# A two-layer and one-block transformer forward pass on one core: dummy matmuls at the start, a split last output, and a reordered recurrent block

## The chip, the cores and the metric

The kernel runs on one core of one Trainium2 chip. The metric is the device time of one execution, in microseconds (us); lower is better. All times below are from profiled or timed executions of the kernel before the change.

## The reference

The input is 256 tokens of width 1024, in float32. Two layers and a further block follow each other. Cut to the part that the change touches:

```
def rg_lru_block(x, w_in, b_in, conv_w, conv_b, gate_w, gate_b, lam, w_out, b_out):
    u = x @ w_in + b_in
    gate_branch, rec = u[..., :1024], u[..., 1024:]
    rec = causal_depthwise_conv(rec, conv_w, conv_b)          # 4 taps
    gl = (block-diagonal product of rec with gate_w) + gate_b # 4 blocks of 256
    r_gate, i_gate = sigmoid(gl[0]), sigmoid(gl[1])
    log_a = -8 * r_gate * softplus(-lam)
    a = exp(log_a);  mult = sqrt(-expm1(2 * log_a))
    h = linear_recurrence(a, mult * (i_gate * rec))           # along the tokens
    return (gelu(gate_branch) * h) @ w_out + b_out

layer 0:  h = x + rg_lru_block(rms_norm(x));  h = h + swiglu_ffn(rms_norm(h))
layer 1:  h = h + stick_breaking_attention(rms_norm(h));  h = h + swiglu_ffn(rms_norm(h))
block 2:  two mixers on rms_norm(h), merged;  h = h + merged @ w_out
          h = h + (p @ w_ple) * sigmoid(h @ w_ple_gate)       # the output
```

## The kernel before

Every weight matrix is read once, in chunks of 128x2048 numbers (1 MB). A chunk is loaded in two halves from SP's queue into `raw`, which has two slots (`RAWS = 2`): the load of chunk c waits until VectorE has finished the same half of chunk c-2 (`lo_dve`). ScalarE copies a half to `whi` (rounded to fp32r; `split_part`, L983), VectorE writes the rest, `wlo = raw - whi` (L1503), and TensorE multiplies with three matmuls per tile (hi x hi, hi x lo, lo x hi). `whi` and `wlo` have four slots. `split_alone` is a split in which VectorE makes the copy too (L1710). Each engine's program is written out by hand, in order; semaphores join them.

Chunks 0 to 3 are `rec` (the recurrent half of `w_in`), 4 `gates_a`, 5 `branch_a`, 6 `gates_b`, 7 to 9 `branch_b`, 10 to 13 `lru_out`, 14 on the first feed-forward part. TensorE takes them in this order. Around the change:

- Start: `x` lands in two halves (`s_x`); squares and roots give a factor for each token; VectorE writes it on diagonals (`diag`, L1561); TensorE multiplies `h` with them, which transposes and scales at once (L583, eight traced matmuls for each of four groups j); ScalarE and VectorE make `xhi` (L1015) and `xlo` (L1535); chunk 0 then goes through TensorE in pairs of k (L448 to L450).
- Parameters: small rows are transposed (`parameters`, L589 and L590), and VectorE computes from them (L1626 to L1644).
- Recurrent block, for each of four groups j of 256 channels: ScalarE `last_tap` (L1079), VectorE `convolve` (L1668, L1677), ScalarE `rec_hi` (L1087), VectorE `conv_lo` (L1690); then for pairs of groups the gates' products on TensorE, ScalarE sigmoids (L1100), Exp and Tanh (`gate_decay`, L1110 and L1116), Sqrt (`gate_root`, L1123), Gelu (`branch_gelu`, L1131); VectorE `gated_input` (L1696), `decay_factor` (L1701), `scan` (L1716, L1719), `output` (L1726); ScalarE `y_hi_of` (L1138), VectorE `output_lo` (L1731). TensorE's `outputs_wide` for `lru_out` waits for `y_lo`, and its second chunk writes banks that the Gelus of groups 2 and 3 read.
- `output_bias` on GpSimd's queue adds `b_out` to `h` with two accumulating DMAs of 512 KB (L430), after `rec` chunk 3.
- End: the last product (`ple_gate`) is followed by Sigmoid (L1481), a product and a sum on VectorE (L2265, L2266) and the DMA to `out` (L419), for tiles of 128x512.

ScalarE's functions come from table sets; a change of set is an instruction of its own (ACT_TABLE_LOAD).

## Time and profile before

| | us |
|---|---|
| median of 3 runs | 847.23 (846.73 to 847.96) |
| the profiled execution's own time | 846.38 |
| its span, from the first to the last instruction | 844.6 |
| TensorE busy in it | 827.6 (98%) |
| VectorE busy | 573.3 (68%) |
| ScalarE busy | 475.5 (56%) |
| DMA | 148.31 MB, mean 176 GB/s |

The span is the stretch that the trace shows; 1.8 us of the execution's time lie around it. Busy shares are averages over the whole span, and the change touches the first 90 us and the last 20.

### The profile page before, as it was taken

Reading aid. Unit: us, or ns where it says so; the run is one execution under the profiler, and the core shown is the slowest. Engines: PE = TensorE matmul, PEld = TensorE weight load, DVE = VectorE, ACT = ScalarE, POOL = GpSimd, SP = SyncE. Lnnn points to the kernel's source line nnn. Section 1 sums busy time; section 2 is a strip of 40 time slices with the busy share of each in tenths; the row PEclk is TensorE's granted clock in tenths of the full one; section 3 lists DMA queues with packets and bytes.
Section 4 is the critical chain, followed back from the end, with each engine's and each line's share of the span. In section 5 each row is a group of like instructions: output and inputs, shape, how many; then the busy total and the mean of one; then the engine's idle time right before and its main releaser. Section 6 shows DMA issues by size and latency. Waiting matters only on the chain.

```text
span 844.6 us, 12734 instructions
## 1 busy us (share of the span) xinstructions
PE 827.6 (98%) x5093; PEld 735.4 (87%) x5093; DVE 573.3 (68%) x825; ACT 475.5 (56%) x674; POOL 2.1 (0%) x6
## 2 busy tenths in 40 slices
PE   5998999999999999999999999999999999999997
PEld 5997888888888899998888888888999999999886
DVE  5979785665644577775765665555757789888763
ACT  6699684444434566655664444435654846577441
POOL 0000000000000000000000000000000000000000
PEclk9999999999999999999999999999999999999999
DMA  8674688656555464344676556555554364444531
GB/s 279 209 208 159 209 254 262 198 177 196 178 193 179 150 200 139 119 142 130 214 230 195 180 177 195 190 186 177 168 180 136 115 199 126 128 147 142 189 119 50
DMA packets 124307, 148.31 MB, mean 176 GB/s; under 512 B 6217, under 2 KB 100953, under 8 KB 124121
## 3 DMA queue, kind: packets, MB, share of 16 engines
q1 hardware_dynamic: 122584, 144.73, 54.0%
q0 software_dynamic: 288, 1.05, 0.8%
q10 hardware_dynamic: 1376, 1.72, 0.7%
q8 instruction: 41, 0.67, 0.3%
q14 instruction: 18, 0.14, 0.1%
HBM read 146.41 MB, written 2.63 MB: 176 GB/s over the span
## 4 chain that ended last, share of the span: by engine, by line
PE 85%; DVE 6%; ACT 5%; DMA 3%; issue 1%; SPq 0%; ACTq 0%; DVEq 0%
PE bank L506 18%; PE bank L508 18%; PE bank L507 18%; PE bank L448 7%; PE bank L449 6%; PE bank L450 6%; DVE wlo L1503 2%; DMA raw<-in_lru_w_in 2%; PE bank L863 2%; PE bank L455 1%; PE bank L457 1%; PE bank L456 1%; ACT whi L983 1%; PE bank L657 1%; PE bank L517 1%
## 5 line engine op out<-in xcount | busy, mean ns | idle before, releaser
L1503 DVE TENSOR_TENSOR wlo<-raw,whi 128x1024 fp32r<-128x1024 f32 (+1 forms) x268 | 314.8, 1212 | 103.0 <-ACT whi L983 102.4
L983 ACT ACTIVATE whi<-raw 128x1024 fp32r<-128x1024 f32 (+1 forms) x266 | 267.0, 1048 | 177.7 <-PE bank L508 103.1
L448 PE MATMUL bank<-xhi,whi 128*128 128x256 f32 x576 | 165.1, 287 | 0.2 <-issue 0.2
L450 PE MATMUL bank<-xhi,wlo 128*128 128x256 f32 x576 | 162.9, 283 | 0.0
L449 PE MATMUL bank<-xlo,whi 128*128 128x256 f32 x576 | 162.9, 283 | 0.0
L506 PE MATMUL bank<-whi,xhi 128*128 128x512 f32 x384 | 151.6, 395 | 0.3
L508 PE MATMUL bank<-whi,xlo 128*128 128x512 f32 x384 | 149.8, 390 | 0.0
L507 PE MATMUL bank<-wlo,xhi 128*128 128x512 f32 x384 | 149.5, 389 | 0.0
L448 PEld LDWEIGHTS bank<-xhi,whi 128*128 128x128 f32 x576 | 110.4, 192 | 1.8 <-issue 1.2
L449 PEld LDWEIGHTS bank<-xlo,whi 128*128 128x128 f32 x576 | 110.5, 192 | 0.1
L450 PEld LDWEIGHTS bank<-xhi,wlo 128*128 128x128 f32 x576 | 110.4, 192 | 0.0
L508 PEld LDWEIGHTS bank<-whi,xlo 128*128 128x128 f32 x384 | 72.1, 188 | 15.3
L506 PEld LDWEIGHTS bank<-whi,xhi 128*128 128x128 f32 x384 | 72.1, 188 | 15.2 <-issue 0.9
L507 PEld LDWEIGHTS bank<-wlo,xhi 128*128 128x128 f32 x384 | 72.2, 188 | 14.4
L506 PE MATMUL bank<-whi,a_ghi 128*128 128x512 f32 x176 | 69.1, 392 | 0.0
L508 PE MATMUL bank<-whi,a_glo 128*128 128x512 f32 x176 | 68.6, 390 | 0.0
L507 PE MATMUL bank<-wlo,a_ghi 128*128 128x512 f32 x176 | 68.5, 389 | 0.0
L1216 ACT ACTIVATE a_sg<-bank,stat 128x256 f32<-128x256 f32 x44 | 18.5, 471 | 65.2 <-PE bank L508 65.2
L1803 DVE SCALAR_TENSOR_TENSOR a_gt<-bank,stat,a_sg 128x256 f32<-128x256 f32 x44 | 19.3, 480 | 47.6 <-ACT a_sg L1216 45.1
L508 PEld LDWEIGHTS bank<-whi,a_glo 128*128 128x128 f32 x176 | 33.0, 188 | 7.0
L506 PEld LDWEIGHTS bank<-whi,a_ghi 128*128 128x128 f32 x176 | 33.0, 188 | 6.7
L507 PEld LDWEIGHTS bank<-wlo,a_ghi 128*128 128x128 f32 x176 | 33.1, 188 | 6.6
(313 smaller groups left out, 1176.6 us busy)
## 6 DMA issues: line engine op xcount, KB each, us to landing
raw<-in_ffn_w_in SPq DMA_DIRECT2D x176, 256.0 KB, 3.6
raw<-in_w_in SPq DMA_DIRECT2D x48, 512.0 KB, 4.7
raw<-in_ffn_w_out SPq DMA_DIRECT2D x44, 512.0 KB, 4.1
raw<-in_attn_w_qkv SPq DMA_DIRECT2D x24, 512.0 KB, 4.6
raw<-in_lru_w_in SPq DMA_DIRECT2D x14, 512.0 KB, 5.3
raw<-in_lru_w_out SPq DMA_DIRECT2D x8, 512.0 KB, 4.0
raw<-in_attn_w_o SPq DMA_DIRECT2D x8, 512.0 KB, 3.9
raw<-in_w_out SPq DMA_DIRECT2D x8, 512.0 KB, 4.6
```

Source lines behind the costliest of these rows:

```text
L448: nc.tensor.matmul(dst, wh, hi, start=start, stop=False, skip_group_check=shared)
L449: nc.tensor.matmul(dst, wh, lo, start=False, stop=False, skip_group_check=shared)
L450: return nc.tensor.matmul(dst, wl, hi, start=False, stop=stop, skip_group_check=shared)
L455: nc.tensor.matmul(dst, hi, wh, start=start, stop=False)
L506: nc.tensor.matmul(dst, hi, wh, start=start, stop=False)
L507: nc.tensor.matmul(dst, hi, wl, start=False, stop=False)
L508: return nc.tensor.matmul(dst, lo, wh, start=False, stop=stop)
L863: last = nc.tensor.matmul(dst, k[:, u * P:(u + 1) * P], queries, start=True, stop=True)
L983: nc.scalar.activation(whi[:, c % RING, part], raw[:, c % RAWS, part], ACT.Copy).then_inc(hi_done, 1)
L1216: nc.scalar.activation(sg[:, q % 2, a, :], bank[(b0 + 2 * q + a) % 4][:, 0:S], ACT.Sigmoid, scale=stat[:, 10 * xn + 8 + a:10 * xn + 9 + a] ...
L1503: nc.vector.tensor_tensor(wlo[:, c % RING, part], raw[:, c % RAWS, part], whi[:, c % RING, part].bitcast(F32), ALU.subtract).then_inc(lo_d ...
L1803: marks.append(mark(nc.vector.scalar_tensor_tensor(out=gt[:, q % 2, a, :], in0=bank[(b0 + 2 * q + a) % 4][:, 0:S], scalar=tok(xn, a), in1= ...
```

## The change

What it does:

- TensorE runs 10 dummy products of a tile of ones before the identity lands and 7 more before the diagonals are ready (`keep_clock`; in the trace a float32 product shows as two matmuls). Of the four transposing groups the last runs between chunk 0's first and second pair of k. The squares at the start are shared out anew: ScalarE takes the first 128 tokens, VectorE the others, each as a half lands.
- Of the 1216 KB of constants only the 50 KB of `bucket` are loaded at their old place; the others (1 MB) go behind the fourth chunk of `ffn_in0`, and `p_tok` behind `gates_b`. `bound_constants` moves into the feed-forward part, and VectorE computes the parameters behind the first half of chunk 1.
- In the recurrent block, Sqrt for all four groups comes once, behind the second `gate_decay`, and Gelu's table stays for all four groups. VectorE alone splits chunks 7 and 8, and ScalarE copies chunk 10 (10 was VectorE's). ScalarE's copy of chunk 6 moves ahead of `last_tap(3)`, and the bucket copy moves to ScalarE.
- The two bias DMAs wait for `rec` chunk 2, not 3.
- The last 128x512 tile of `ple_gate` is computed, activated, added and stored in two halves of 256 columns.

The diff, cut to its core:

```diff
                     if layer == 0 and c == 3:
+                        sp.dma_start(const[:, 256:CONST["bucket"]], t["consts"][:, 256:CONST["bucket"]])\
+                            .then_inc(s_const, 16)
...
-            sp.dma_start(p_tok[:, :, :], t["p_2"][0, 0].rearrange("(a p) d -> p a d", p=P))\
-                .then_inc(s_p, 16)
-            sp.dma_start(const[:, 256:], t["consts"][:, 256:]).then_inc(s_const, 16)
+            bucket = slice(CONST["bucket"], CONST["bucket"] + 384)
+            sp.dma_start(const[0:33, bucket], t["consts"][0:33, bucket]).then_inc(s_bucket, 16)
             stage("rec", lambda c: w_in[4 + c], 2)
...
-                pool.wait_ge(chunk_done, STAGES["rec"][0] + 3 + 5)
+                pool.wait_ge(chunk_done, STAGES["rec"][0] + 2 + 5)
...
+            def keep_clock(n):
+
+                for _ in range(n):
+                    nc.tensor.matmul(bank[5][:, 0:P], rs[:, 0:P], rs[:, 0:P], start=True, stop=True)
+
+            pe.wait_ge(warm_ready, 1)
+            keep_clock(10)
+            pe.wait_ge(s_ident, 16)
+            pe.wait_ge(s_gain, 16)
+            nc.tensor.transpose(bank[4][:, 0:16], prow[0:16, 0, :], ident[0:16, 0:16]).then_inc(gain_t, 1)
+            keep_clock(7)
+            pe.wait_ge(tok_ready, 1)
+            for j in range(3):
+                first_transposes(j)
...
-            columns_part(c0, b0, xhi, xlo, 0, 4, x_lo, 0)
+            columns_part(c0, b0, xhi, xlo, 0, 2, x_lo, 0)
+            first_transposes(3)
+            columns_part(c0, b0, xhi, xlo, 2, 4, x_lo, 0)
             parameters()
             columns_part(c0, b0, xhi, xlo, 4, DT, x_lo, 0)
...
+            def gate_half(c, half):
+
+                dst = bank[4 + half][:, 0:S]
+                for k in range(4):
+                    kk = 4 * (c - 2) + k
+                    xh, xl = xhi[:, kk, P:], xlo[:, kk, P:]
+                    wh, wl = (w[:, (c0 + c) % RING, k * WIDE + half * S:k * WIDE + (half + 1) * S] for w in (whi, wlo))
+                    nc.tensor.matmul(dst, xh, wh, start=kk == 0, stop=False)
+                    nc.tensor.matmul(dst, xh, wl, start=False, stop=False)
+                    last = nc.tensor.matmul(dst, xl, wh, start=False, stop=kk == DT - 1)
+                return last
...
+            nc.scalar.preload_act_table_set("sigmoid_and_others")
             last_tap(0)
             split(3)
             rec_hi(0)
             last_tap(1)
+            act.wait_ge(bkt_t, 1)
+            nc.scalar.activation(bucket_bias[:, :], bank[7][0:8, 0:384], ACT.Copy).then_inc(bkt_done, 1)
             split(4)
             rec_hi(1)
+            act.wait_ge(bkt_done, 1)
+            act.dma_start(bias_dram, bucket_bias[:, :]).then_inc(bkt_out, 16)
             last_tap(2)
             split(5)
             rec_hi(2)
+            split(6)
             last_tap(3)
-            act.wait_ge(bkt_done, 1)
-            act.dma_start(bias_dram, bucket_bias[:, :]).then_inc(bkt_out, 16)
-            split(6)
-            nc.scalar.preload_act_table_set("sigmoid_and_others")
             gate_sigmoids("gates_a", 0)
+            rec_hi(3)
             nc.scalar.preload_act_table_set("exp_and_others")
-            rec_hi(3)
-            split(7)
             gate_decay(0)
-            gate_root(0)
-            split(8)
             nc.scalar.preload_act_table_set("sigmoid_and_others")
             gate_sigmoids("gates_b", 2)
+            act.wait_ge(hi_done, parts_done(8, 2))
             split(9)
             gate_decay(2)
+            gate_root(0)
+            gate_root(2)
             nc.scalar.preload_act_table_set("gelu_apprx_tanh_and_others")
             branch_gelu(STAGES["branch_a"][0], 0)
             c0 = STAGES["branch_b"][0]
             branch_gelu(c0, 1)
+            split(10)
             act.wait_ge(bkt_out, 16)
             y_hi_of(0)
             y_hi_of(1)
-            gate_root(2)
-            act.wait_ge(hi_done, parts_done(10, 2))
             split(11)
-            nc.scalar.preload_act_table_set("gelu_apprx_tanh_and_others")
             branch_gelu(c0 + 1, 2)
             branch_gelu(c0 + 2, 3)
...
+            split_part(1, 0)
             dve.wait_ge(par_t, 1)
...
-            split(1)
+            split_part(1, 1)
             split(2)
...
-            lru_constants()
-            dve.wait_ge(bkt_t, 1)
-            nc.vector.tensor_copy(bucket_bias[:, :], bank[7][0:8, 0:384]).then_inc(bkt_done, 1)
             convolve(1)
             split(4)
             conv_lo(1)
             convolve(2)
             split(5)
             conv_lo(2)
+            lru_constants()
             convolve(3)
             split(6)
             conv_lo(3)
-            split(7)
+            split_alone(7)
             gated_input(0)
             gated_input(1)
             decay_factor(0)
             decay_factor(1)
-            scan(0)
-            split(8)
-            scan(1)
+            split_alone(8)
             gated_input(2)
             gated_input(3)
             split(9)
-            split_alone(10)
             decay_factor(2)
             decay_factor(3)
+            scan(0)
             output(0)
+            scan(1)
             output(1)
+            split_part(10, 0)
             output_lo(0)
             output_lo(1)
+            split_part(10, 1)
             scan(2)
...
+                    if n and a:
+                        for half in range(2):
+                            part = slice(half * S, (half + 1) * S)
+                            cols = slice(WIDE + half * S, WIDE + (half + 1) * S)
+                            dve.wait_ge(pg_sig, 4 + half)
+                            link(nc.vector.tensor_tensor(xg[:, 1, part], xg[:, 1, part], ple[:, 1, cols], ALU.mult))
+                            nc.vector.tensor_tensor(h[:, 1, cols], h[:, 1, cols], xg[:, 1, part], ALU.add)\
+                                .then_inc(fin_ready, 1)
+                        continue
```

The rows below are the program order, first of **ScalarE** from the third `rec_hi` to the gates' Exp and Tanh (a_rchi is `rec_hi`, a_rc<-bank `last_tap`, whi<-raw a chunk's copy, a_rg and a_ig the sigmoids, then a_av_lru Exp and a_rg Tanh). Before:

```order
L1087 ACTIVATE a_rchi<-a_rc 128x512
L1079 ACTIVATE a_rc<-bank,small,par 128x256 x2
L1151 DMA bias_scratch<-a_bucket_bias 8x384
L983 ACTIVATE whi<-raw 128x1024 x2
L1153 ACT_TABLE_LOAD
L1100 ACTIVATE a_rg<-bank,par 128x256 x4
L1100 ACTIVATE a_ig<-bank,par 128x256 x4
L1155 ACT_TABLE_LOAD
L1087 ACTIVATE a_rchi<-a_rc 128x512
L983 ACTIVATE whi<-raw 128x1024 x2
L1110 ACTIVATE a_av_lru<-a_rg,small 128x256 x4
L1116 ACTIVATE a_rg<-a_rg,small 128x256 x4
```

And in the changed kernel:

```order
L1131 ACTIVATE a_rchi<-a_rc 128x512
L1026 ACTIVATE whi<-raw 128x1024 x2
L1123 ACTIVATE a_rc<-bank,small,par 128x256 x2
L1144 ACTIVATE a_rg<-bank,par 128x256 x4
L1144 ACTIVATE a_ig<-bank,par 128x256 x4
L1131 ACTIVATE a_rchi<-a_rc 128x512
L1202 ACT_TABLE_LOAD
L1154 ACTIVATE a_av_lru<-a_rg,small 128x256 x4
L1160 ACTIVATE a_rg<-a_rg,small 128x256 x4
L1204 ACT_TABLE_LOAD
L1144 ACTIVATE a_rg<-bank,par 128x256 x4
```

Chunk 6's copy now stands ahead of the fourth `last_tap` instead of behind it, the table load between them is gone, and so is chunk 7's copy ahead of Exp; the second gates' sigmoids follow at once, without Sqrts ahead of them.

**VectorE** behind the last `convolve` (wlo is the rest of a chunk, CAST a chunk's copy on this engine, a_rclo `conv_lo`, a_ig `gated_input`, then `decay_factor`, a_rg and the a_ig behind it `scan`). Before:

```order
L1503 TENSOR_TENSOR wlo<-raw,whi 128x1024 x2
L1690 TENSOR_TENSOR a_rclo<-a_rc,a_rchi 128x512
L1503 TENSOR_TENSOR wlo<-raw,whi 128x1024 x2
L1696 TENSOR_TENSOR a_ig<-a_ig,a_rc 128x512 x2
L1701 SCALAR_TENSOR_TENSOR a_ig<-a_av_lru,a_ig 128x512 x2
L1716 TENSOR_TENSOR a_rg<-a_rg,a_ig 128x512
L1719 SCALAR_TENSOR_TENSOR a_ig<-a_av_lru,a_rg 128x256 x2
L1503 TENSOR_TENSOR wlo<-raw,whi 128x1024 x2
L1716 TENSOR_TENSOR a_rg<-a_rg,a_ig 128x512
L1719 SCALAR_TENSOR_TENSOR a_ig<-a_av_lru,a_rg 128x256 x2
L1696 TENSOR_TENSOR a_ig<-a_ig,a_rc 128x512 x2
L1503 TENSOR_TENSOR wlo<-raw,whi 128x1024 x2
```

And in the changed kernel:

```order
L1558 TENSOR_TENSOR wlo<-raw,whi 128x1024 x2
L1757 TENSOR_TENSOR a_rclo<-a_rc,a_rchi 128x512
L1777 CAST whi<-raw 128x1024
L1558 TENSOR_TENSOR wlo<-raw,whi 128x1024
L1777 CAST whi<-raw 128x1024
L1558 TENSOR_TENSOR wlo<-raw,whi 128x1024
L1763 TENSOR_TENSOR a_ig<-a_ig,a_rc 128x512 x2
L1768 SCALAR_TENSOR_TENSOR a_ig<-a_av_lru,a_ig 128x512 x2
L1777 CAST whi<-raw 128x1024
L1558 TENSOR_TENSOR wlo<-raw,whi 128x1024
L1777 CAST whi<-raw 128x1024
L1558 TENSOR_TENSOR wlo<-raw,whi 128x1024
```

Chunks 7 and 8 now each bring two CASTs into VectorE's order, and the two scans have moved away, behind the rows shown.


## Rows read from the trace of the kernel before

**Rows 1.** The page: busy us, share of the span, instructions.

```profile
PE 827.6 (98%) x5093; PEld 735.4 (87%) x5093; DVE 573.3 (68%) x825; ACT 475.5 (56%) x674; POOL 2.1 (0%) x6
```

**Rows 2.** Timeline of TensorE: start us, us, what, count, [idle before <-releaser].

```profile
8.64 5.39 PE L583 MATMUL bank<-diag,h 128*128 128x128 f32 x32 [2.54 <-DVE diag L1561]
...
20.46 0.36 PE L448 MATMUL bank<-xhi,whi 128*128 128x256 f32 x1 [0.23 <-issue]
...
75.65 0.47 PE L506 MATMUL bank<-whi,a_yhi 128*128 128x512 f32 x1 [1.76 <-DVE a_ylo L1731]
...
82.88 0.47 PE L506 MATMUL bank<-whi,a_yhi 128*128 128x512 f32 x1 [1.51 <-ACT a_gel L1131]
```

**Rows 3.** The chain that ended last, at the start: start us, us, what.

```profile
1.23 5.32 DMA h<-in_x
...
8.64 2.09 PE bank L583 x8
10.82 0.85 ACT xhi L1015 x2
11.77 0.88 DVE xlo L1535 x2
```

**Rows 4.** Only L583: stretch, us, busy (count) of PE and PEld, PEclk, DMA share, GB/s.

```profile
9.10:11.10 2.00, 2.00 (x11) 2.00 (x11) 1.00 0.37 120
12.20:13.60 1.40, 1.40 (x15) 1.40 (x14) 1.00 1.08 322
```

**Rows 5.** The same of all lines, PE, PEld, DVE, ACT, POOL.

```profile
30.00:40.00 10.00, 10.00 (x86) 10.00 (x85) 9.73 (x26) 5.10 (x8) 0.48 (x1) 1.00 0.55 182
825.00:835.00 10.00, 10.00 (x46) 8.29 (x45) 3.08 (x5) 1.20 (x2) 0.00 (x0) 1.00 0.15 54
```

**Rows 6.** Timeline of VectorE.

```profile
17.20 0.28 DVE L1626 COPY par<-bank 128x122 f32<-128x122 f32 x1 [0.40 <-PE bank L590]
19.15 2.35 DVE L1503 TENSOR_TENSOR wlo<-raw,whi 128x1024 fp32r<-128x1024 f32 x2
...
24.34 0.16 DVE L1668 TENSOR_TENSOR a_rc<-a_rc,diag 128x6 f32<-128x6 f32 x1
...
42.66 2.43 DVE L1677 SCALAR_TENSOR_TENSOR a_rc<-bank,par,a_rc 128x255 f32<-128x255 f32 x6
45.01 2.36 DVE L1503 TENSOR_TENSOR wlo<-raw,whi 128x1024 fp32r<-128x1024 f32 x2
...
58.52 1.27 DVE L1719 TENSOR_TENSOR_SCAN a_ig<-a_av_lru,a_rg 128x256 f32<-128x256 f32 x2
...
67.86 0.69 DVE L1710 CAST whi<-raw 128x1024 fp32r<-128x1024 f32 x1
```

**Rows 7.** DMA of 42 to 44 us: queue, packets, MB, share of 16 engines.

```profile
q0 software_dynamic: 78, 0.32, 105.8%
```

**Rows 8.** The chain that ended last, in the recurrent block.

```profile
41.98 9.35 DMA raw<-in_lru_w_in
```

**Rows 9.** DMA of 40 to 41.5 us: issues, KB each, median us to landing.

```profile
h<-in_lru_b_out POOLq DMA_DIRECT2D x2, 512.0 KB, 8.0
raw<-in_lru_w_in SPq DMA_DIRECT2D x1, 512.0 KB, 7.4
```

**Rows 10.** Timeline of ScalarE in the recurrent block.

```profile
54.04 1.71 ACT L1116 ACTIVATE a_rg<-a_rg,small 128x256 f32<-128x256 f32 x4
55.77 1.28 ACT L1123 ACT_TABLE_LOAD   x1
...
81.06 1.57 ACT L1131 ACTIVATE a_gel<-bank,par 128x256 f32<-128x256 f32 x4
```

**Rows 11.** Timeline of GpSimd's queue.

```profile
39.52 1.90 POOL L430 DMA_DIRECT2D h<-in_lru_b_out  x2 [39.08 <-PE bank L450]
```

**Rows 12.** The chain that ended last, at the end.

```profile
840.08 0.61 ACT xg L1481
841.43 0.69 DVE h L2266
```

More of the change, by code:

```diff
@@ L415, in _ @@
             out_v = out[0].rearrange("(a p) d -> p a d", p=P)
-            for j in range(4):
+            for j in range(3):
                 cols = slice(j // 2 * WIDE, (j // 2 + 1) * WIDE)
@@ L585, in _ @@
                 last.then_inc(chunk_done, 1)
+            pe.wait_ge(warm_ready, 1)
[5 more added lines that the diff above has]
+            pe.wait_ge(tok_ready, 1)
+            for j in range(3):
+                first_transposes(j)
             def parameters():
@@ L958, in _ @@
                         pe.wait_ge(banks_read, b0 + c + a + 1)
+                    if c >= 2 and a == 1:
+                        for half in range(2):
+                            last = gate_half(c, half)
+                            if c == 3 and half == 0:
+                                last.then_inc(pg_mm, 1)
+                        continue
                     last = gate_part(c, a, 0, 4)
@@ L1476, in _ @@
                         act.wait_ge(pg_mm, n + 1)
-                    else:
-                        act.wait_ge(chunk_done, c0 + 2 * n + 1 + 5)
+                    elif n == 0:
+                        act.wait_ge(chunk_done, c0 + 1 + 5)
                     if n:
                         act.wait_ge(fin_ready, a + 1)
+                    if n and a:
+                        for half in range(2):
+                            cols = slice(half * S, (half + 1) * S)
+                            if half:
+                                act.wait_ge(chunk_done, c0 + 3 + 5)
+                            else:
+                                act.wait_ge(pg_mm, 3)
+                            nc.scalar.activation(xg[:, 1, cols], bank[4 + half][:, 0:S], ACT.Sigmoid)\
+                                .then_inc(pg_sig, 1)
+                        continue
                     nc.scalar.activation(xg[:, a, :], bank[(b0 + 2 * n + a) % 4][:, :], ACT.Sigmoid)\
@@ L1844, in ffn @@
                         norm_factor(xn)
-                        if layer:
+                        if not layer:
+                            bound_constants()
+                        else:
                             link(nc.vector.tensor_tensor(two_gains, gains("final_norm"), gains("norm_gain"),
@@ L2263, in _ @@
                 for a in range(2):
+                    if n and a:
+                        for half in range(2):
+                            part = slice(half * S, (half + 1) * S)
+                            cols = slice(WIDE + half * S, WIDE + (half + 1) * S)
+                            dve.wait_ge(pg_sig, 4 + half)
+                            link(nc.vector.tensor_tensor(xg[:, 1, part], xg[:, 1, part], ple[:, 1, cols], ALU.mult))
+                            nc.vector.tensor_tensor(h[:, 1, cols], h[:, 1, cols], xg[:, 1, part], ALU.add)\
+                                .then_inc(fin_ready, 1)
+                        continue
                     dve.wait_ge(pg_sig, 2 * n + a + 1)
```

62 lines of the change are left out of this document (39 added, 23 removed).

## The prediction

> **What bounds the kernel now.** The page first: TensorE is busy 98% of the span [rows 1]. So a gain can come only from a stretch in which it waits, from a slower clock, or from the tail behind its last matmul. Its timeline shows these stretches [rows 2]: nothing but one small product before 8.64 us, idle time of 0.23 us at 20.46, 1.76 us at 75.65 (it waits for the first y_lo) and 1.51 us at 82.88 (for the Gelus that read its banks). The chain at the start says what 8.64 rests on: the DMA of x [rows 3], which no edit touches. The transposing products run at two rates. Of L583 alone [rows 4], 11 matmuls touch 2.0 us early on, each 0.42 us long, so one every (2.0 + 0.42) / 11 = 0.22 us; later 15 touch 1.4 us at 0.28 us each, one every 0.11 us. These are the clock's two levels, 1.2 and 2.4 GHz. The PEclk column says 1.00 in both, so the counts are what shows it. After that a 256-column matmul takes (10.0 + 0.28) / 86 = 0.120 us and a 512-column one 0.23 us [rows 5].
>
> **Start.** The ten dummy products are 20 traced matmuls, 20 x 0.21 = 4.3 us from about 1.0 us on; the seven behind the row transposition (about 5.9 us) are 14, so 1.6 us at the fast level, 3.0 at the slow. In before the level rose 15 matmuls, 3.2 us, after 8.64. I expect it up before the diagonals are there. Then the first eight products end at about 9.8 us, where before xhi could start only at 10.82; with ScalarE's 0.85 and VectorE's 0.88 [rows 3] chunk 0 starts at 11.8, where it started at 13.78 = 8.64 + 5.14. It takes 48 x 0.12 = 5.75, the fourth transposing group 0.9 in its midst and the parameters' transpositions 0.5, so it ends at 18.95. Before it ended at about 20.1, the wait at 20.46 behind it. **1.1 us gained** here. In chunk 1 VectorE makes the first half (1.2 us), then the parameter block, 19.15 - 17.20 = 1.95 us [rows 6], then the second half: ready at 20.5, wanted 12 matmuls into the chunk, at 20.4. The 0.36 us of before become 0.1. Chunk 1 ends at 24.7; the bias table takes 0.8 and chunk 2 5.75, to 31.3 us, against 32.9.
>
> If the clock stayed low, the first xhi would come at the old time, the dummies would last to about 9.2 us and hold the transposes back by 0.6, and the fourth group and the waits between would cost in full: chunk 0 would end near 21.7.
>
> **The constants.** 1.2 MB leave the queue ahead of chunk 2, which at the 322 GB/s of the start [rows 4] is 3.5 us of transfer. That is covered now by ScalarE: its copies of chunk 2 wait for the parameters (VectorE, 19.3), four small functions 0.8, copies 2.0, a table 1.28, `last_tap` 0.9, so `convolve(0)` starts at 24.1 against 24.34 [rows 6]. Loaded later, 1 MB goes beside feed-forward chunks of 24 x 0.227 = 5.45 us each, split up to three chunks ahead: some 3 us against 16 us of cover. I take nothing for it; without the cover it would cost up to 3 us.
>
> **The recurrent block up to the fourth group.** `lru_constants` and the bucket copy leave VectorE ahead of `convolve(1)`: it starts 2.54 + 2.28 + 0.6 = 5.4 us behind `convolve(0)` (the first two are 45.01 - 42.47, with the small addition of 0.19 ahead of row 42.66, and two halves' wlo), at 29.5, and ends at 32.05. The first wlo half of chunk 4 is done at 33.2, which releases the first load of chunk 6 (`gates_b`); the second goes 1.1 us later, at 34.4.
>
> This is where the moved wait bites. The bias DMAs were issued 0.9 us after chunk 3 [rows 11], so now at 31.3 + 0.9 = 32.2 us. Each takes 8.0 us to land [rows 9]. Between 42 and 44 us the software queue alone held 105.8% of the engines' time [rows 7], and chunk 7's first half, issued about 1.3 us behind the bias DMAs, took 7.4 us [rows 9], its second, issued at 41.98, 9.35 us [rows 8]. So it landed 41.98 + 9.35 - 39.52 = 11.8 us after the bias DMAs' start. Now chunk 6 stands in chunk 7's place: issued 1.0 and 2.2 us behind them. Its second half lands at 32.2 + 11.5 = 43.7 us (0.3 less, being issued 0.3 sooner behind them). In before ScalarE met chunk 7 off the critical chain of the convolutions; now the copy of chunk 6 stands ahead of `last_tap(3)`: 43.7 + 1.05 + 0.9 gives `convolve(3)` at C = 45.7, against 42.47. What is queued behind: `last_tap(3)`, all gate sigmoids, a_rchi; who waits: VectorE, and through a_rclo TensorE at `gates_b` (2 us).
>
> At that place a rule bears on it. The Trainium skill, DMA: Bandwidth & Descriptors, section "Queues, rings and completion order", says that a DMA engine takes turns between queues, a packet each. The row of 42 to 44 us shows 78 software packets and none of the other queue's; by the rule the halves would come earlier (rival 2).
>
> **From there to the outputs.** Counted from C: VectorE's convolution, chunk 6 and a_rclo 5.4; chunk 7 alone 2 x (0.72 + 1.14) = 3.7 (the CAST and what follows it [rows 6]); four 128x512 operations 2.9; chunk 8's second copy 2.6. That releases ScalarE, which is behind it: chunk 9 2.0, table 1.28, Exp and Tanh 3.45, table 1.28, four Sqrts 2.1, table 1.28, first Gelus 0.8 [rows 10] = 12.2. Then VectorE: y 0.7, a scan 0.7 + 1.3 [rows 6], y 0.7, half a chunk 1.1, y_lo 0.7 = 5.2. With hand-overs y_lo(0) is there at C + 32.1 = 77.8. Before it was 75.55 - 42.47 = 33.1: two table loads (2.6) and two chunks' copies less on ScalarE, but 2.8 us more copying on VectorE now lie in the chain, so it shortens by only 1.0. TensorE, through with `branch_b` at 74.2, stands from there to 77.9.
>
> It then has 5.45 us of work, to 83.3 (before it restarted at 82.88), and needs no Gelu: the fourth one is done at C + 33.6. The second chunk takes it to 88.8, but y_lo(2) comes at C + 43.5 = 89.2 (two scans 4.1, four half chunks less one 3.4, two y 1.4, y_lo 0.7 behind C + 33.9). Before it was there at 82.88 + 5.45 = 88.3. **0.9 us lost.** From here on TensorE is dense in both.
>
> **End.** The halves cost 48 x 0.120 - 24 x 0.227 = +0.3 us of TensorE. The tail, 841.43 + 0.69 - 840.08 = 2.04 us [rows 12], becomes three operations of half width. Bounds for each: half of 0.6 or 0.69, and the whole; I take 0.47 and 0.45 twice, 1.4 us. The last store moves half the bytes; 0.1 for it. **0.4 us gained.**
>
> **Sum.** 846.38 + 0.9 - 0.4 = 846.9 us by the profiled execution. The runs' median of 847.23 lies 0.85 above that one, so **847.7 us** as a median. A measurement of this kernel tells no change from about 0.2%, 1.7 us.
>
> **Rivals.**
> 1. Chunk 6 is not late: the bias DMAs start later, or chunk 6's loads get through before them. For it: only 1 us separates them. Against: chunk 7's load in before, in the same place, was starved. Then C = 41.0 (VectorE-bound: 32.05 + 2.9 + 2.5 + 3.5), y_lo(0) at 73.1, and TensorE is at y_lo(2) at 84.5: 3.8 gained and 0.4 at the end, 843.0. Chance 0.22.
> 2. The queues share, and the second half lands at 41 to 42.5: C = 43 to 44.4, so 1.3 to 2.7 us under the forecast, 845.0 to 846.4; middle 845.7. Chance 0.20, half of it faster by over 0.2%.
> 3. The clock falls in the wait of 3.7 us ahead of y_lo(0). In before the longest wait inside, 1.8 us, left it up. Until it rises again, as at the start for 3.2 us, half the work is lost: 1.6 us, so 849.3, slower. It decides if the wait is long enough for the chip. Chance 0.08. The Trainium skill, TensorE: Matmul & The Clock Gate, section "Why this matters for your kernels", warns of just such gaps between bursts of matmuls.
> 4. The dummies don't raise the clock. Chunk 0 ends 2.8 us later than forecast, the bias DMAs move along with it, and all to y_lo(2) is 2.8 us later: 850.5, slower. For it: a pause of 0.5 us at 5.4 and one of 1 us before 8.64. Chance 0.07.
>
> **Chances.** The forecast has 0.43, its own range 846.4 to 849.3 (C by 1 us either way, the tail by 0.4); of it 0.32 within 0.2%, 0.07 slower, 0.04 faster. Faster: 0.22 + 0.10 + 0.04 = 0.36. Same: 0.32 + 0.10 = 0.42. Slower: 0.07 + 0.08 + 0.07 = 0.22. The range leaves out most of rival 4 and the far ends: 842.4 to 849.7.
>
> **What would show it.** Right: the transposing products at one every 0.11 us from 8.64, chunk 0 starting near 11.8; the bias DMAs issued near 32.2, chunk 6's second half 9 us in flight, ScalarE idle 5 us ahead of its copy; one wait of over 3 us on y_lo, none on a Gelu; a tail of 1.4 us. The forecast is wrong if chunk 6 lands before 41 us, if VectorE reaches chunk 4's wlo over 1 us sooner than 33.2, or if the slow clock lasts into chunk 0.

## Result, and the profile after

The changed kernel takes 849.31 us (median of 11 runs, 848.25 to 850.26), the kernel before 847.23 in the same session: ratio 1.0023, 95% interval 1.0016 to 1.0031, slower by 0.23%. The forecast was 847.7 with 842.4 to 849.7, so the time lies in the range, near its slow end. The profiled execution took 850.19 us with a span of 848.1, so it lies 0.9 above its median, as that of before lay 0.85 below; of the 3.5 us between the two spans, 2.1 stand in the medians.

TensorE's waits of the changed kernel, longest first (where it waited, for whom; total us, times, longest):

```profile
PE bank L458 <- issue: 2.5, 1, 2.5
PE bank L516 <- DVE a_ylo L1798: 2.2, 1, 2.2
PE bank L587 <- DVE rs L1669: 1.1, 1, 1.1
PE bank L594 <- DVE diag L1616: 0.9, 1, 0.9
PE bank L602 <- DMA a_prow<-in_mix_norm: 0.7, 1, 0.7
PE bank L516 <- DVE a_gt L1874: 0.7, 1, 0.7
```

Against [rows 2]: the wait for the Gelus is gone, the one for y_lo(0), the low part of the block's output for group 0, is 2.2 instead of 1.76, and two are new inside the kernel: 2.5 us ahead of `gates_b` (L458), and 0.7 us ahead of the feed-forward's fifth chunk (L516, for a_gt, its first gated product, which VectorE makes from the same banks). Where the waits at `gates_b` and for y_lo(0) come from, the timelines of ScalarE, then of VectorE show (start, duration, operation, in brackets the idle time ahead and its releaser):

```profile
44.55 1.06 ACT L1026 ACTIVATE whi<-raw 128x1024 fp32r<-128x1024 f32 x1 [3.36 <-DMA raw<-in_lru_gate_w]
45.52 1.00 ACT L1123 ACTIVATE a_rc<-bank,small,par 128x256 f32<-128x256 f32 x2
...
46.62 0.17 DVE L1735 TENSOR_TENSOR a_rc<-a_rc,diag 128x6 f32<-128x6 f32 x1 [5.23 <-ACT a_rc L1123]
49.17 2.35 DVE L1558 TENSOR_TENSOR wlo<-raw,whi 128x1024 fp32r<-128x1024 f32 x2
78.17 1.29 DVE L1798 TENSOR_TENSOR a_ylo<-a_rc,a_yhi 128x512 fp32r<-128x512 f32 x2
```

The same two operations of VectorE in the kernel before, the start of `convolve(3)` and y_lo(0):

```profile
42.47 0.16 DVE L1668 TENSOR_TENSOR a_rc<-a_rc,diag 128x6 f32<-128x6 f32 x1
...
74.81 1.29 DVE L1731 TENSOR_TENSOR a_ylo<-a_rc,a_yhi 128x512 fp32r<-128x512 f32 x2
```

ScalarE stands 3.36 us for the second half of chunk 6, the copy takes 1.06, `last_tap(3)` behind it starts at 45.5, `convolve(3)` at 46.62 instead of 42.47. Chunk 6's low parts follow it and are done at 51.5, which is what TensorE waits for at `gates_b`; y_lo(0) starts at 78.17 instead of 74.81. The DMA view says why. Of 33.6 to 35 us, chunk 6's two loads (KB each, median us to landing); under it the queues of 38 to 44 us (packets, MB, share of the engines' time), the software queue being that of the bias transfers:

```profile
raw<-in_lru_gate_w SPq DMA_DIRECT2D x2, 512.0 KB, 8.0
...
q1 hardware_dynamic: 1152, 1.15, 56.8%
q0 software_dynamic: 151, 0.52, 44.2%
```

The clock. TensorE's busy time, matmuls and granted clock by stretch (start:end, us, busy us and count, clock, DMA share, GB/s):

```profile
51.70:55.00 3.30, 3.30 (x16) 0.50 0.91 290
55.20:58.50 3.30, 3.30 (x30) 1.00 0.83 239
79.00:82.40 3.40, 3.40 (x8) 0.50 0.69 202
83.00:86.40 3.40, 3.40 (x17) 1.00 0.53 181
```

After each of the two waits the clock stands at its lower level, 1.2 GHz, for 3.4 us; at the second, 8 matmuls of 512 columns are done in the time of 15 to 17. The output product (`lru_out`), from the start of its first matmul to that of its last, takes 23.8 us, where the kernels without a fall and without a wait for Gelus take 22.1 to 22.5.

The other new wait lies where the constants now load. ScalarE ahead of its copies of the feed-forward's fifth chunk, behind which its sigmoids for a_gt stand in its order; TensorE ahead of that chunk; and the DMA issues of 106 to 112 us, with those of 95 to 104 us last:

```profile
118.55 1.06 ACT L1026 ACTIVATE whi<-raw 128x1024 fp32r<-128x1024 f32 x1 [3.58 <-DMA raw<-in_ffn_w_in]
...
127.32 0.47 PE L516 MATMUL bank<-whi,xhi 128*128 128x512 f32 x1 [0.67 <-DVE a_gt L1874]
...
raw<-in_ffn_w_in SPq DMA_DIRECT2D x6, 256.0 KB, 6.2
const<-in_consts SPq DMA_DIRECT2D x1, 1024.0 KB, 8.0
...
raw<-in_ffn_w_in SPq DMA_DIRECT2D x7, 256.0 KB, 4.2
```

In every trace with the constants loaded at this place ScalarE stands for this load. Where it stood 3.2 us or more (3.58 here, 3.69 in number 12, 3.19 in number 11) TensorE had to wait for a_gt; where it stood 1.1 to 2.3 us, as in the others, it had not.

Start and end of the changed kernel:

```profile
8.45 2.94 PE L594 MATMUL bank<-diag,h 128*128 128x128 f32 x24 [0.93 <-DVE diag L1616]
11.68 0.36 PE L458 MATMUL bank<-xhi,whi 128*128 128x256 f32 x1 [0.29 <-DVEq L1688]
...
844.51 0.38 ACT L1533 ACTIVATE xg<-bank 128x256 f32<-128x256 f32 x1 [0.99 <-PE bank L988]
845.38 0.42 DVE L2340 TENSOR_TENSOR h<-h,xg 128x256 f32<-128x256 f32 x1
```

The transposing products run at one every 0.12 us from the first on (2.94 / 24), and the last sigmoid is followed by 1.29 us to the sum's end (845.38 + 0.42 - 844.51) instead of 2.04 [rows 12].

The sum of the differences between the two profiled spans: lru_out starts 3.35 us later (79.00 against 75.65); through it 0.2 is won (no 1.5 us for the Gelus, 1.3 more for the clock's fall); the a_gt wait and its restart cost 0.9; the halves cost TensorE 0.4; the stretch from the last matmul's end to the span's is 3.6 instead of 4.55, 0.95 shorter. 3.35 - 0.2 + 0.9 + 0.4 - 0.95 = 3.5, the whole difference.

### The profile page after: what moved, and what is told of

It reads as the page before. It is cut to its first block, busy times and chain, and to the rows that moved or that the text cites. A ratio compares the mean times of both kernels' runs of the same rounds, so it can differ in the third digit from the quotient of the medians.

```text
span 848.1 us, 12860 instructions
## 1 busy us (share of the span) xinstructions
PE 835.4 (99%) x5151; PEld 743.3 (88%) x5151; DVE 575.1 (68%) x831; ACT 471.3 (56%) x670; POOL 2.1 (0%) x6
## 4 chain that ended last, share of the span: by engine, by line
PE 84%; DVE 8%; ACT 4%; DMA 3%; issue 1%; SPq 0%; DVEq 0%; ACTq 0%
PE bank L516 17%; PE bank L518 17%; PE bank L517 17%; PE bank L458 7%; PE bank L459 6%; PE bank L460 6%; DVE wlo L1558 3%; PE bank L888 2%; PE bank L465 1%; PE bank L466 1%; PE bank L467 1%; DMA raw<-in_lru_gate_w 1%; PE bank L680 1%; PE bank L527 1%; ACT whi L1026 1%
## 5 line engine op out<-in xcount | busy, mean ns | idle before, releaser
L458 PE MATMUL bank<-xhi,whi 128*128 128x256 f32 x576 | 165.2, 287 | 0.5 <-DVEq L1688 0.3
L516 PE MATMUL bank<-whi,xhi 128*128 128x512 f32 x376 | 148.6, 395 | 1.0 <-DVE a_gt L1874 0.7
L518 PE MATMUL bank<-whi,xlo 128*128 128x512 f32 x376 | 146.7, 390 | 0.0
L517 PE MATMUL bank<-wlo,xhi 128*128 128x512 f32 x376 | 146.5, 390 | 0.0
L458 PEld LDWEIGHTS bank<-xhi,whi 128*128 128x128 f32 x576 | 110.3, 192 | 2.2 <-ACT whi L1026 0.6
L516 PEld LDWEIGHTS bank<-whi,xhi 128*128 128x128 f32 x376 | 70.6, 188 | 15.9 <-ACT whi L1026 1.1
L516 PE MATMUL bank<-whi,a_ghi 128*128 128x512 f32 x176 | 69.1, 392 | 0.0
L516 PEld LDWEIGHTS bank<-whi,a_ghi 128*128 128x128 f32 x176 | 33.0, 188 | 6.7
```

The lines of the kernel that those rows point to most:

```text
L458: nc.tensor.matmul(dst, wh, hi, start=start, stop=False, skip_group_check=shared)
L516: nc.tensor.matmul(dst, hi, wh, start=start, stop=False)
L517: nc.tensor.matmul(dst, hi, wl, start=False, stop=False)
L518: return nc.tensor.matmul(dst, lo, wh, start=False, stop=stop)
```

## Experiments

They ran four kernels at a time on one chip, each beside the kernel before, whose medians there were 847.26 (numbers 1 to 4), 847.47 (5 to 8) and 847.59 (9 to 12). Theory: the moved wait of the bias transfers starves chunk 6 and the rest follows. Rivals: the copies that VectorE took over, the new order of ScalarE's work, the constants, the start and the end.

**1. The wait back at chunk 3 (bias_c3).**

```diff
-                pool.wait_ge(chunk_done, STAGES["rec"][0] + 2 + 5)
+                pool.wait_ge(chunk_done, STAGES["rec"][0] + 3 + 5)
```

> The changed kernel with one wait back in its old place: the two bias transfers wait for recurrent chunk 3 again, not for chunk 2. My theory (the bias transfers, issued at 32.5 us, take the DMA engines from chunk 6's weights, whose second half lands at 44.5; ScalarE stands 3.4 us for it, so convolve(3) starts at 46.6 and not at 42.5, and all of the recurrent chain after it is late): chunk 6's second half lands by 39, convolve(3) starts at 42 to 43.5, TensorE's wait ahead of gates_b is under 0.5 us and the clock doesn't fall there, y_lo(0) comes at 74 to 75.5, and the output product starts there and not at 79.0: 849.3 - 3.5 = 845.8 us (844 to 846.8). The clock may still fall in the wait ahead of y_lo(0), since TensorE is there earlier too. Rival, that VectorE's two more copies and the new order of ScalarE's work make the chain long: convolve(3) comes earlier and y_lo(0) doesn't, 849.3 (848.6 to 850).

Measured 846.71 us, ratio 0.9997 (0.9987 to 1.0007). The 2.5 us wait is gone and y_lo(0) starts 2.6 us earlier, but the transfers now hit chunk 7, and VectorE, which copies it, waits; TensorE stands 3.7 us for y_lo(0), and its clock falls there for 3.4 us:

```profile
51.28 0.69 DVE L1777 CAST whi<-raw 128x1024 fp32r<-128x1024 f32 x1 [2.27 <-DMA raw<-in_lru_w_in]
...
76.39 0.77 PE L516 MATMUL bank<-whi,a_yhi 128*128 128x512 f32 x1 [3.67 <-DVE a_ylo L1798]
```

So the wait is a cause, and its old place is no good one either once VectorE needs chunk 7 itself. I had expected 0.9 us less.

**2. The wait at chunk 6 (bias_c6).**

```diff
-                pool.wait_ge(chunk_done, STAGES["rec"][0] + 2 + 5)
+                pool.wait_ge(chunk_done, STAGES["gates_b"][0] + 5)
```

> The changed kernel with the two bias transfers waiting for chunk 6 (TensorE's second gates, some 54 us), behind every load of the recurrent block's start. My theory: as with the wait at chunk 3, 845.8, and up to 0.5 us less, since chunk 7's and 8's loads are free of them only here if those matter (chunk 7 isn't waited for in the changed kernel's trace, so I take nothing for it): 845.6 (844 to 846.8). If the bias transfers are only put beside another load that is waited for (chunks 9 to 12, of which the changed kernel waits 0.2 us for one): 847 to 849. Rival of the long chain: 849.3.

Measured 843.31 us (842.95 to 843.77), ratio 0.9954 (0.9941 to 0.9966): 6.0 us off the changed kernel by one constant, 2.3 more than the theory gave, since I had overlooked chunk 7. `convolve(3)` and y_lo(0) (VectorE), then TensorE's only wait in the block:

```profile
41.97 0.17 DVE L1735 TENSOR_TENSOR a_rc<-a_rc,diag 128x6 f32<-128x6 f32 x1 [0.34 <-ACT a_rc L1123]
73.52 1.28 DVE L1798 TENSOR_TENSOR a_ylo<-a_rc,a_yhi 128x512 fp32r<-128x512 f32 x2
...
74.35 0.47 PE L516 MATMUL bank<-whi,a_yhi 128*128 128x512 f32 x1 [1.49 <-DVE a_ylo L1798]
```

The clock stays up. The bias transfers now run beside a load for lru_out that nobody is short of: issued at 57.9 us it lands at 67.8.

**3. `last_tap(3)` ahead of `split(6)` (tap_first).**

```diff
+            last_tap(3)
             split(6)
-            last_tap(3)
```

> The changed kernel with last_tap(3) ahead of split(6) on ScalarE again, the bias transfers as in the changed kernel. Chunk 6 still lands at 44.5, but convolve(3) no longer stands behind it: it starts at 42 to 42.5, the low parts of chunk 6 are ready at 46.9, and TensorE's wait ahead of gates_b is gone with the clock's fall there. ScalarE's sigmoids still stand behind chunk 6's high part and come only 0.9 us earlier. If the chain goes by ScalarE's sigmoids (gates_a): y_lo(0) 0.9 us earlier, 848.4. If it goes by VectorE (the copies of chunk 8, for which ScalarE waits 1.3 us at split(9) in the changed kernel, and which come 4 us earlier): y_lo(0) 1.9 to 2.8 us earlier, 847.0 (846.3 to 847.6). If the order was no matter: 849.3.

Measured 847.36 us, ratio 0.9998 (0.9989 to 1.0007), nearest the VectorE case. The wait at `gates_b` is gone though chunk 6 lands as late as before, y_lo(0) starts 2.5 us earlier, and TensorE waits 3.8 us for it. The order of two ScalarE operations was worth 1.9 us, but only because the load between them was late. Here the clock stayed down longer than anywhere else: the granted clock is 0.50 from 75.5 us on, while TensorE still waits, and until 82.2, 6.8 us in all:

```profile
76.50:82.10 5.60, 5.60 (x13) 0.50 0.57 187
83.00:86.40 3.40, 3.40 (x17) 1.00 0.54 183
```

**4. Work in the two waits (fill).** 16 traced matmuls of 128 columns that nobody reads (FILL is 8, and each product shows as two), ahead of `gates_b` and again ahead of lru_out:

```diff
+                if n0:
+                    pe.wait_ge(gate_read, 1)
+                    for _ in range(FILL):
+                        nc.tensor.matmul(bank[4][:, 0:P], rs[:, 0:P], rs[:, 0:P], start=True, stop=True)
...
+            pe.wait_ge(gate_read, 8)
+            for _ in range(FILL):
+                nc.tensor.matmul(bank[7][:, 0:P], rs[:, 0:P], rs[:, 0:P], start=True, stop=True)
```

> The changed kernel with 16 added 128x128 products whose result nobody reads (1.8 us of TensorE) in each of the two waits, ahead of gates_b and ahead of the output product, so that TensorE isn't idle for long there; nothing that anyone waits for is moved. It takes away the clock's two falls alone. If the falls cost what they seem to (each 3.4 us at half speed, 1.7 us of work): the first is taken back in the wait that follows, since TensorE then stands for y_lo(0) anyway; the second comes straight off the end: 849.3 - 1.7 = 847.6 (847.2 to 848.2), and half level shows nowhere but at the start and the end. If the first also holds up ScalarE's sigmoids of gates_b (it waits 0.6 us for TensorE there): 0.6 less, 847.0. If the falls cost nothing: 849.3.

Measured 848.38 us (847.75 to 849.43), ratio 1.0016 (1.0007 to 1.0025): 0.9 us back, of 1.7 expected. The clock is at its upper level in both places, and lru_out takes 22.5 us again. But the first group did not do what I meant: it stood behind a semaphore of its own, so it ran only after a wait of 2.27 us, and put `gates_b` off to 53.2:

```profile
51.40 2.02 PE L642 MATMUL bank<-rs 128*128 128x128 f32 x16 [2.27 <-issue]
...
76.73 1.95 PE L678 MATMUL bank<-rs 128*128 128x128 f32 x16
...
79.00:82.40 3.40, 3.40 (x16) 1.00 0.68 204
```

The third line is the stretch in which the changed kernel did 8. The second fall is thus worth 1.3 us in the profile; the medians show 0.9 for both groups together. The two profiled executions are 2.4 us apart, but 0.9 of that is the wait for a_gt, which this one hasn't.

**5 and 6. The wait alone, in the kernel before (before_bias_c2, before_bias_c6).** There it stood at chunk 3.

```diff
-                pool.wait_ge(chunk_done, STAGES["rec"][0] + 3 + 5)
+                pool.wait_ge(chunk_done, STAGES["rec"][0] + 2 + 5)
```

> The kernel before with one wait changed: the two bias transfers wait for recurrent chunk 2 instead of 3; everything else as before. It tells whether the earlier bias transfers alone lose what the changed kernel lost. My theory: chunk 6's second half lands at 44 to 45 instead of under 41; in this kernel last_tap(3) stands ahead of split(6), so convolve(3) stays at 42.5, but ScalarE waits some 2.4 us for chunk 6, and its sigmoids and all behind them come 1.4 us later (chunk 7, for which it waited 0.96 us, comes earlier). y_lo(0) at 77 instead of 75.65, TensorE waits 3.2 us for it: 848.6; since the clock fell in waits of 2.2 to 3.8 us in the runs so far and not in one of 1.8 us, it falls here, some 1 to 1.7 us more: 850.0 (848.3 to 850.6). Rival, that the early transfers cost only because of the changed kernel's new order: 847.2 (846.8 to 847.6).

Measured 849.85 us, ratio 1.0028 (1.0019 to 1.0037). ScalarE waits 2.6 us for chunk 6's second half, and one of the two waits of TensorE moves: 2.2 us for a_rclo at `gates_b`, after which the clock falls, and 0.6 for y_lo(0). So the earlier bias transfers alone lose what the whole change lost (2.4 us against 2.1).

> The kernel before with the two bias transfers waiting for chunk 6 (TensorE's second gates) instead of recurrent chunk 3; everything else as before. It tells how much of the 843.3 us of the changed kernel with that wait is the wait's and not the change's. My theory: in the kernel before the bias transfers hit chunk 7, for which ScalarE waits 0.96 us at 50.4; without that wait y_lo(0) comes 0.96 us earlier, 1.0 us off TensorE's wait of 1.8: 847.2 - 1.0 = 846.3 (845.8 to 846.8), and the other 3 us of the 843.3 are the change's own. Rival, that the transfers cost the kernel before nothing (the 0.96 us are taken back by another wait of the chain): 847.2. Rival, that nearly all of it is the wait's: 843.5 to 845.

Measured 845.92 us, ratio 0.9981 (0.9973 to 0.999). The wait for y_lo(0) went from 1.8 to 0.6. Of the 3.9 us by which bias_c6 was under the kernel before, 1.5 are thus the wait's place in that kernel and 2.4 the rest of the change. The two don't simply add: by the medians, each against the kernel before of its own session, the rest of the change is worth 0.3 us with the wait at chunk 2 (+2.4 against +2.1), 0.5 at chunk 3 (not clear of noise) and 2.4 at chunk 6.

**7. The end alone (end_only): the kernel before with the last sigmoids, products, sums and stores in halves.**

```diff
+                    if c >= 2 and a == 1:
+                        for half in range(2):
+                            last = gate_half(c, half)
...
-            for j in range(4):
+            for j in range(3):
+            for half in range(2):
+                cols = slice(WIDE + half * S, WIDE + (half + 1) * S)
```

> The kernel before with one part of the change alone: the last gate chunks' second token block in two halves of 256 columns, so that the last sigmoid, product, sum and store are half as wide. Forecast before the result: TensorE 0.3 us longer, the tail 0.6 shorter, the store 0.1: 847.2 - 0.4 = 846.8. From the changed kernel's trace: the last matmul ends 3.6 us before the end instead of 4.55 (0.95 less), TensorE 0.3 us longer: 847.2 - 0.65 = 846.6 (846.3 to 846.9). Rival, that the halves are paid with a wait at the end: 847.2 or more.

Measured 846.55 us, ratio 0.9987 (0.9978 to 0.9996): 0.9 under the 847.47 of its session. The interval runs from 0.3 to 1.9 us, so it shows a gain but can't tell the 0.6 of the traces from the forecast's 0.4.

**8. One more chunk for VectorE (vec9): bias_c6, and chunk 9's high part copied by VectorE too.**

```diff
-            act.wait_ge(hi_done, parts_done(8, 2))
-            split(9)
             gate_decay(2)
...
-            split(9)
+            split_alone(9)
             decay_factor(2)
```

> The changed kernel with the bias transfers waiting for chunk 6 (843.3 us) and one more chunk whose high part VectorE copies: chunk 9, beside 7 and 8. ScalarE's chain is then free of 2.0 us of copies and of the 0.6 us that it waits for VectorE ahead of them. My theory of the chain (from 58 us on it goes by ScalarE: decay, roots, gelu; TensorE stands 1.5 us for y_lo(0) at its end): y_lo(0) comes 2.0 to 2.6 us earlier, at 71 instead of 73.5, TensorE no longer waits for it: 843.3 - 1.5 = 841.8 (841.4 to 842.2). Rival, that VectorE is the chain's bound there (it takes 1.4 us more, ahead of decay_factor(2)): y_lo(0) 1.4 us later, 844.7. Rival, that the low parts of chunk 9 come too late for TensorE (1.4 us later, at 63 us, when TensorE wants them at 65): 843 to 844.

Measured 841.07 us (840.91 to 841.65), ratio 0.9925 (0.9911 to 0.9939), the fastest with number 10. TensorE's wait of 1.5 us is gone, as forecast. y_lo(0) starts at 70.9, and TensorE waits for nothing from 21 us to the feed-forward:

```profile
70.89 1.29 DVE L1797 TENSOR_TENSOR a_ylo<-a_rc,a_yhi 128x512 fp32r<-128x512 f32 x2
...
70.00:76.00 6.00, 6.00 (x38) 1.00 0.52 168
```

**9 to 12. Parts of the change undone in vec9**, where the start and the chain show at the end undisturbed. What they show holds for vec9, where no load of the block is late, and not at once for the changed kernel. They ran in another session than vec9.

9, the 17 products that nobody reads left out (v9_no_dummies):

```diff
-            keep_clock(10)
...
-            keep_clock(7)
```

> The last kernel (bias transfers at chunk 6, VectorE copies chunk 9 too: 841.1 us; TensorE waits for nothing between 21 us and the end of the block, so that what the start loses or gains shows at the end) without the 17 products that nobody reads at TensorE's start. In the kernel before the clock rose 2.8 us after TensorE's first real products; here it would rise at 11.3 us instead of at 4 us, so that the first transposes run at half speed from 8.45 us on: up to 1.5 us lost. The sum on record took 1.1: 842.2 (841.8 to 842.8). If the first chunk's start is set by the arrival of the high and low parts and not by the clock: 841.1 to 841.4.

Measured 842.80 us (842.22 to 843.29), 1.7 over vec9, the far end of what I gave. The first transposing products of this kernel, of vec9, of the kernel before, of before_bias_c2 and of end_only, each with its duration:

```profile
8.57 5.38 PE L594 MATMUL bank<-diag,h 128*128 128x128 f32 x24 [2.41 <-DVE diag L1613]
...
8.59 2.94 PE L594 MATMUL bank<-diag,h 128*128 128x128 f32 x24 [0.65 <-DVE diag L1615]
...
8.64 5.39 PE L583 MATMUL bank<-diag,h 128*128 128x128 f32 x32 [2.54 <-DVE diag L1561]
...
8.56 6.78 PE L583 MATMUL bank<-diag,h 128*128 128x128 f32 x32 [2.59 <-DVE diag L1561]
...
8.88 6.44 PE L587 MATMUL bank<-diag,h 128*128 128x128 f32 x32 [2.69 <-DVE diag L1593]
```

The start of the last three is the same code, and it takes 5.4 or 6.4 to 6.8 us: when the clock rises differs from one execution to the next. With the added products it is up before the real ones in every trace (2.94 us for 24, in all of the nine kernels that have them). In the two traces chunk 0 starts 1.9 us apart (13.71 and 11.82), and so does all behind it. The spread of the runs doesn't follow the added products: bias_c3, which has them, spreads over 3.4 us, this kernel without them over 1.1, vec9 over 0.7.

10, the 1 MB of constants back ahead of recurrent chunk 2 (v9_const_early):

```diff
-                    if layer == 0 and c == 3:
-                        sp.dma_start(const[:, 256:CONST["bucket"]], t["consts"][:, 256:CONST["bucket"]])\
...
+            sp.dma_start(const[:, 256:CONST["bucket"]], t["consts"][:, 256:CONST["bucket"]]).then_inc(s_const, 16)
             stage("rec", lambda c: w_in[4 + c], 2)
```

> The last kernel with the 1 MB of constants loaded early again, ahead of recurrent chunk 2's weights (issued at 12 us, as in the kernel before). The prediction on record took 'constants loaded later' as free. If that is right, chunk 2's first half lands at 19 to 20 instead of 16.1 and still in time (TensorE wants it at 24): 841.1 (840.8 to 841.5). Rival, that loading them later is what gives the chain its start (ScalarE's taps and so the convolutions stand behind chunk 2's high part, which ScalarE then waits for): the chain to y_lo(0) starts up to 1 us later, but has 1.1 us of slack here: 841.1 to 841.6. Rival, that TensorE itself waits for chunk 2: 842 to 843.

Measured 841.01 us (840.82 to 841.05), no difference. The feed-forward's loads beside which the constants no longer run land in 3.6 us (8 issues of 100 to 108 us), where the 8 of vec9 in the same stretch take 6.2. The five runs spread over 0.2 us, where two of vec9's five lie 0.6 above the others; whether those two had the wait for a_gt no trace shows.

11, chunks 7 and 8 copied by ScalarE again (v9_act78):

```diff
+            split(7)
             gate_decay(0)
+            split(8)
...
-            split_alone(7)
+            split(7)
...
-            split_alone(8)
+            split(8)
```

> The last kernel with the high parts of chunks 7 and 8 copied by ScalarE again, in the places of the kernel before (chunk 9 stays with VectorE). ScalarE has 4.0 us more ahead of gates_b's decay, 1.8 us of which lie in its waits for TensorE there: its chain comes 2.2 us later, y_lo(0) at 73.1 instead of 70.9, and TensorE, which wants it at 72.6, waits 0.9 us (to the operation's end): 841.1 + 0.9 = 842.0 (841.5 to 842.8). If VectorE were the bound of that chain, it would be 2.8 us shorter and the time no longer: 841.1.

Measured 843.01 us (842.88 to 843.2), 1.9 over vec9. y_lo(0) starts at 73.06, as worked out, and TensorE's output product starts 1.3 us later than in vec9. What I hadn't in the sum: it also takes 0.4 longer, and 0.5 is lost at the wait for a_gt (0.3), beside the constants. VectorE's copies, the chief rival for the loss, are a gain here.

12, roots and Gelus in their old places, and the first two scans back around VectorE's chunk 8 (v9_old_roots; the scans are not in the cut):

```diff
             gate_decay(0)
+            gate_root(0)
...
             gate_decay(2)
-            gate_root(0)
-            gate_root(2)
...
             y_hi_of(1)
+            gate_root(2)
             split(11)
+            nc.scalar.preload_act_table_set("gelu_apprx_tanh_and_others")
```

> The last kernel with the roots and the GELUs in the places of the kernel before: root(0) right after decay(0), root(2) behind y_hi(1), and the table of the GELUs loaded once more behind it, with scan(0) and scan(1) around VectorE's chunk 8. It undoes 'roots and GELUs once per table'. ScalarE's chain to y_lo(0) loses a table load and two roots (3.5 us) and has 0.6 us more ahead of gates_b's sigmoids: y_lo(0) comes 2 to 3 us earlier, where TensorE doesn't wait for it; the second group of GELUs comes 0.8 us later, at 74.6, ahead of TensorE's need at 78. So no difference: 841.1 (840.8 to 841.5). Rival, that grouping them is what took away the 1.5 us wait for a_gel of the kernel before: it comes back, 842.5.

Measured 841.57 us (841.01 to 842.28), ratio 0.9926 (0.9914 to 0.9937). Its median is 0.5 over vec9's, but against the kernel before the two are alike (0.9926 and 0.9925). Its runs lie in two groups, about 841.1 and 842.1. The profiled execution is of the slower kind and has no wait in the block, but the one for a_gt (0.7 us), with ScalarE short of feed-forward weights beside the constants as in the changed kernel:

```profile
PE bank L516 <- DVE a_gt L1874: 0.7, 1, 0.7
...
110.92 1.06 ACT L1026 ACTIVATE whi<-raw 128x1024 fp32r<-128x1024 f32 x1 [3.69 <-DMA raw<-in_ffn_w_in]
```

In this trace the wait with its restart costs 1.0 of the 1.4 us over vec9's, and the output product takes 0.3 longer. So the grouping itself is worth nothing that shows here; that the slower runs are those with the wait for a_gt is not shown. Not undone by themselves were the parameters' and `p_tok`'s new places.

## Why the prediction was right or wrong

**The moved wait** was right in mechanism and nearly in size. The bias transfers were issued at 32.5 us (forecast 32.2), chunk 6's second half landed at 44.5 (43.7), 9.7 us after its issue, and `convolve(3)` started at 46.6 (45.7). Numbers 1, 2, 5 and 6 show it from both sides: the wait moved from chunk 3 to chunk 2 alone gives +2.4 us in the kernel before and +2.6 in the changed one (846.71 to 849.31), and from chunk 2 to chunk 6 -6.0 in the changed one.

**From C to y_lo(0)** I had 32.1 us to its end. To its start it is 31.55, in the changed kernel (46.62 to 78.17) and in bias_c6 (41.97 to 73.52) alike, and it takes 0.69 more: 32.2. That the chain goes by ScalarE behind chunk 8 was confirmed by number 8; for its way by VectorE up to there speaks number 3, which came out nearest that case.

**The clock** is the step of the sum that failed. The sum took it to stay at its upper level in both waits, the 2 us at `gates_b` and the 3.7 us ahead of y_lo(0); only rival 3, with a chance of 0.08, had it fall in the second ("It decides if the wait is long enough for the chip"). It fell in both, after 2.5 and 2.2 us. The first fall cost `gates_b` 1.6 us (7.3 us from its start to the next product, 5.8 in before), paid out of the second wait, which shrank from 3.7 to 2.2. The second cost 1.3 us (the rival had 1.6) and put TensorE behind y_lo(2), for which I had it wait 0.4. So of the signs that I named one failed: there was no wait of over 3 us on y_lo. The Trainium skill, TensorE: Matmul & The Clock Gate, section "Why this matters for your kernels", warned of idle gaps between bursts of matmuls. The trace agrees that they lower the clock, but here gaps of 2.2 and 2.5 us were enough, shorter than those the page warns of.

**Queues sharing** (rival 2) didn't hold: in 38 to 44 us the software queue's 151 packets held 44.2% of the engines' time and the other's 1152 only 56.8%, so a software packet costs (44.2 / 151) / (56.8 / 1152) = 5.9 times as much as one of the other queue. Taking turns by packets, as the Trainium skill, DMA: Bandwidth & Descriptors, section "Queues, rings and completion order", has it, would then still leave chunk 6 a small part of the time. In 41 to 42 us the trace agrees: 40 software packets held 81.8% and 41 of the other queue 15.4%. In 35 to 36 us, right behind chunk 6's issues, it doesn't: 45 against 5. My reading of the rule as an even share was wrong in both.

**The constants**, taken as free, cost 0.9 us in the profiled execution (0.67 of wait and the restart) and nothing in most other traces: the cover, "some 3 us against 16", was counted in chunks ahead, but there ScalarE waits for one feed-forward load after the other, even in vec9, where TensorE doesn't notice it. Loading them early costs nothing in vec9 (number 10). The 3.5 us of transfer that the prediction had for them at the start is 3.7 by its own numbers (1.2 MB at 322 GB/s); nothing hangs on it.

**The start** came as forecast between the two profiled executions: chunk 0 starts at 11.68 (11.8), and chunk 2 1.3 us earlier than in before (25.82 against 27.12), where the sum had 1.1 behind chunk 0 and 1.6 behind chunk 2. What I couldn't see in one trace is that the start without the added products has more than one length: chunk 0 starts at 13.8 and 13.7 us in before and before_bias_c6, but at 15.1 in before_bias_c2 and end_only. The profile that I worked from has a short one. So against a median of starts the gain is larger (number 9 has 1.7), and the 0.85 us that I added to come from one execution to the median is unsettled: it may have been in good part the start, which the changed kernel no longer has. That split is not shown.

**The end** gained 0.6 in the traces (0.4 lost on TensorE, 0.95 gained behind it) and 0.9 in number 7, against 0.4: the stretch behind the last matmul was 0.2 better than I had it.

Together, in the profiled executions: the sum had 846.9, it was 850.19, 3.3 more. Of this 1.1 are the later start of the output product (79.0 against 77.9), 1.1 the clock less the wait for y_lo(2) with its restart (through that product +3.15 us against before, where the sum had +0.9), 0.9 the constants, -0.2 the end, and 0.3 lie outside the spans (2.1 against 1.8). In the medians 1.6 remain, since the execution of before lay 0.85 below its median and that of the changed kernel 0.9 above. What differs between that one and its median no run tells; the constants' wait of 0.9, which not every trace has, is the nearest candidate. Rival 1, 843.0 if chunk 6 is not late, is nearly what bias_c6 then measured, 843.3, with `convolve(3)` at 42.0 where the rival had 41.0.

That the time lies in the range is partly luck. It is at the very end of what the forecast's own line allowed (846.4 to 849.3), and the range reached 849.7 for the rivals' sake. Rival 3's 849.3 meets the median, but by terms that cancel: the output product started 1.1 us later than it had, while the 0.85 us for the median was not there.

## What to carry to other kernels

A wait that only decides when a background transfer starts has a price and a gain that depend on which load it meets; look which loads are in flight for the 10 us behind it, and put it beside one that nobody is short of (6 us by one constant here). One profiled execution is one draw: where two traces of the same code differ (the start here by 1.3 us), a sum on one of them carries that. When a chain is made shorter by giving an engine other work, list anew who waits for which load. And where a forecast holds a TensorE wait as long as those in which the clock fell here, put its price into the sum and not into a rival.

## What was not expected of the hardware

- The clock fell in or right behind waits of 2.19, 2.23, 2.5, 3.7 and 3.8 us and stayed up in waits of 1.5, 1.8, 1.9 and 2.27 us (number 4), so the length of the wait alone doesn't decide it. In before_bias_c2 it was still at its upper level when TensorE restarted at 55.4 us and fell 0.3 us later. Each time it stood at the lower level for 3.4 us, once for 6.8 (number 3).
- The clock's rise without the added products comes at different times: 32 transposing products took 5.34, 5.39, 6.44 and 6.78 us in four traces with the same start (before_bias_c6, before, end_only, before_bias_c2), 24 took 5.38 in number 9.
- Two accumulating transfers of 512 KB on GpSimd's queue slow what is issued 1.2 and 2.4 us behind them: chunk 6's two loads, 512 KB each, took 6.3 and 9.7 us, median 8.0, and 4.3 in the median without them (bias_c6).
